# Expert weights of a two-model kernel loaded as three 2 MB transfers into three slots instead of six of 1 MB into six

## What is computed

```python
def expert_block(args):
    xblk, e = args
    return (jax.nn.silu(xblk @ w1[e]) * (xblk @ w3[e])) @ w2[e]
```

## Time and profile before

| | |
|---|---|
| median of three runs | 2905.9 us (2905.66 to 2909.65) |
| profiled execution, its own time | 2905.86 us |
| span of the profile | 2904.0 us |
| TensorE busy, matmuls | 2310.4 us, 80% |
| VectorE busy | 1070.7 us, 37% |
| ScalarE busy | 686.9 us, 24% |
| mean granted clock of TensorE | 0.900 |
| moved | 718.82 MB, mean 248 GB/s |
| share of the chain that ended last: DMA `raw<-in_w` | 24% |

### The profile page before, as it was taken

One profiled execution on the slowest core, in us unless ns is written; L12 is line 12 of the kernel. 1 busy time (PEld: TensorE's weight loads), 2 busy tenths in 40 slices (PEclk: granted clock), 3 DMA queues, 4 the chain that ended last, 5 costly groups with the idle time before them and its releaser, 6 DMA issues.

```text
span 2904.0 us, 35200 instructions
## 1 busy us (share of the span) xinstructions
PE 2310.4 (80%) x13750; PEld 1590.7 (55%) x13750; DVE 1070.7 (37%) x1570; ACT 686.9 (24%) x876; POOL 117.8 (4%) x209
## 2 busy tenths in 40 slices
PE   5998679979987699699558777877369668888885
PEld 5888478878885688587523333332355523333332
DVE  4555545555556355723420100010668410000011
ACT  3334433333335233321101000100335200000100
POOL 0001000000010000000000000000100000000000
PEclk9999789989998799899669999999679788998898
DMA  7775137757752287422149999999420269999997
GB/s 260 261 238 173 56 118 266 253 190 266 262 169 88 104 288 259 139 78 94 73 161 401 399 396 400 402 400 404 179 71 1 87 258 397 401 399 401 401 402 303
DMA packets 242628, 718.82 MB, mean 248 GB/s; under 512 B 17040, under 2 KB 156560, under 8 KB 189072
## 3 DMA queue, kind: packets, MB, share of 16 engines
q1 hardware_dynamic: 213584, 642.82, 59.7%
q10 hardware_dynamic: 19952, 48.45, 4.6%
q0 software_dynamic: 8976, 25.90, 3.0%
HBM read 693.70 MB, written 25.26 MB: 248 GB/s over the span
## 4 chain that ended last, share of the span: by engine, by line
PE 55%; DMA 26%; DVE 9%; issue 4%; DVEq 2%; ACT 2%; SPq 1%; ACTq 0%; POOL 0%; POOLq 0%
DMA raw<-in_w 24%; PE ps L620 13%; PE ps L621 12%; PE ps L622 12%; PE ps L934 10%; PE ps L655 2%; PE ps L634 1%; SPq L554 1%; PE ps L936 1%; PE ps L1071 1%; DVE t_lo L1537 1%; PE ps L1086 1%; DMA raw<-in_ffn_w_up 1%; DVE work L1601 1%; DMA work<-expert_rows,slot_of_token 1%
## 5 line engine op out<-in xcount | busy, mean ns | idle before, releaser
L1537 DVE TENSOR_TENSOR w_lo<-raw,w_hi 128x2048 fp32r<-128x2048 f32 x180 | 411.4, 2290 | 445.1 <-ACT w_hi L1128 445.1
L620 PE MATMUL ps<-t_hi,w_hi 128*128 128x256 f32 (+1 forms) x1568 | 456.4, 291 | 8.7 <-DVE t_lo L1537 8.6
L621 PE MATMUL ps<-t_lo,w_hi 128*128 128x256 f32 (+1 forms) x1568 | 454.1, 290 | 0.0
L622 PE MATMUL ps<-t_hi,w_lo 128*128 128x256 f32 (+1 forms) x1568 | 451.1, 288 | 0.0
L1128 ACT CAST w_hi<-raw 128x2048 fp32r<-128x2048 f32 x180 | 342.1, 1903 | 447.5 <-PE ps L622 428.5
L934 PE MATMUL ps<-raw,work 128*64 128x512 f32 x528 | 308.8, 742 | 167.0 <-DMA raw<-in_w 165.6
L2015 DVE COPY work<-ps 128x512 f32<-128x512 f32 x64 | 44.3, 692 | 932.6 <-PE ps L952 932.6
L620 PE MATMUL ps<-w_hi,t_hi 128*128 128x256 f32 (+1 forms) x1088 | 349.8, 322 | 15.3 <-DVE t_lo L1537 12.4
L622 PE MATMUL ps<-w_hi,t_lo 128*128 128x256 f32 (+1 forms) x1088 | 351.1, 323 | 0.0
L621 PE MATMUL ps<-w_lo,t_hi 128*128 128x256 f32 (+1 forms) x1088 | 351.0, 323 | 0.0
L620 PEld LDWEIGHTS ps<-t_hi,w_hi 128*128 128x128 f32 x1568 | 296.6, 189 | 30.4 <-issue 13.2
(11 more groups left out here) (280 smaller groups left out, 2159.1 us busy)
## 6 DMA issues: line engine op xcount, KB each, us to landing
raw<-in_w SPq DMA_DIRECT2D x256, 1024.0 KB, 11.3
work<-in_w SPq DMA_DIRECT2D x128, 1024.0 KB, 10.7
work<-in_w_mod SPq DMA_DIRECT2D x32, 1536.0 KB, 6.5
raw<-in_ffn_w_gate SPq DMA_DIRECT2D x44, 1024.0 KB, 8.8
raw<-in_ffn_w_up SPq DMA_DIRECT2D x44, 1024.0 KB, 10.3
raw<-in_ffn_w_down SPq DMA_DIRECT2D x44, 1024.0 KB, 4.9
raw<-in_w_in SPq DMA_DIRECT2D x18, 1024.0 KB, 5.5
expert_rows<-work ACTq DMA_DIRECT2D x128, 128.0 KB, 7.2
```

The costliest lines, as they stand in the source:

```text
L620: pe.matmul(dst, a[0], b[0], start=start, stop=False)
L621: pe.matmul(dst, a[0], b[1], start=False, stop=False)
L622: return pe.matmul(dst, a[1], b[0], start=False, stop=stop)
L1537: return dve.tensor_tensor(dst, src, hi.bitcast(F32), ALU.subtract)
```

## The change

The six slots of 1 MB become three of 2 MB: two from the four slots of `raw`, for w1 and w3, and one from the two in the work area, for w2. Each matrix is one transfer. SyncE waits once for the two up matrices, until the whole up product of the expert before is done (`up_done`), and once for w2, until the down product of the expert before that one in w2's order is done (`down_done`). TensorE waits once for both up matrices and once for w2; the order of its products, `expert_done` and what the other engines do are the same. The first four panels of the stage behind a loop wait for the whole last up product.

```diff
-RAW_UP = 6
+RAW_UP = 3
...
         def expert_raw(m, x):
-            return raw[:, (SPLIT_PANELS[m] + x) % RAW, :] if x < RAW else w(R3 + (x - RAW) * KD * PC, KD * PC)
+            if x < 2:
+                return raw[:, 2 * x:2 * x + 2, :].rearrange("p s n -> p (s n)")
+            return w(R3, 2 * KD * PC)
...
+        def up_done(b):
+            return 6 * b + 2 if not isinstance(b, int) or b else 4
+        def down_done(b):
+            return 6 * b + 10 if not isinstance(b, int) or b < EXPERTS - 1 else 6 * b + 6
...
-                    sp.wait_ge(expert_done, MAIN - 6 + j - G0["odd"] + 1)
+                    sp.wait_ge(expert_done, MAIN - 4)
...
-                for j in range(4):
-                    first_load(j, part((w1, w3)[j % 2], 0, j // 2))
-                for j in range(2):
-                    first_load(4 + j, part((w1, w3)[j % 2], 1, 0))
-                for j in (2, 3):
-                    expert_load(up_panel(1, j), up_slot(1, j), part((w1, w3)[j % 2], 1, 1))
-                down_loads(0, 0)
+                def load_matrix(x, wt, e, landed_in):
+                    return sp.dma_start(expert_raw(m, x).rearrange("p (a n) -> p a n", a=1), wt[:, bass.ds(e, 1), :]
+                                        ).then_inc(landed_in, 16)
+                def up_loads(e):
+                    sp.wait_ge(expert_done, MAIN * m + up_done(e - 1))
+                    for x, wt in enumerate((w1, w3)):
+                        load_matrix(x, wt, e, expert_landed[x])
+                def down_load(e):
+                    sp.wait_ge(expert_done, MAIN * m + down_done(e - 1))
+                    load_matrix(2, w2, e, expert_landed[2])
+                sp.wait_ge(w_ready, SPLIT_PANELS[m])
+                for x, wt in enumerate((w1, w3)):
+                    load_matrix(x, wt, 0, expert_landed[x])
+                sp.wait_ge(row_ready, TILE0[10 + 2 * m])
+                load_matrix(2, w2, 0, expert_landed[2])
+                up_loads(1)
                 with sp.Fori(2, EXPERTS) as e:
-                    up_loads(e, None)
-                    down_loads(e - 1, None)
-                down_loads(EXPERTS - 1, EXPERTS - 1)
+                    up_loads(e)
+                    down_load(e - 1)
+                down_load(EXPERTS - 1)
...
-                        pe.wait_ge(expert_landed[x1], count(block))
-                        pe.wait_ge(expert_landed[x3], count(block))
+                        if h == 0:
+                            pe.wait_ge(expert_landed[0], count(b))
+                            pe.wait_ge(expert_landed[1], count(b))
...
+                    pe.wait_ge(expert_landed[2], count(b))
                     for h in range(2):
-                        x = down_slot(y, h)
-                        pe.wait_ge(expert_landed[x], count(EXPERTS - 1 if y == EXPERTS - 1 else b + 1))
-                        down_half(par, h, expert_raw(m, x)).then_inc(expert_done, 1)
+                        down_half(par, h, expert_raw(m, 2)[:, h * 2048:(h + 1) * 2048]).then_inc(expert_done, 1)
```

More of the change, by code:

```diff
@@ L545, in moe @@
                 w2 = A["w2_2"][m].rearrange("e (p c) n -> p e (c n)", c=4)
[L547 to L561, removed]
@@ L563, in up_loads @@
-                def up_loads(e, x):
-                    for j in range(4):
[L565 to L571, removed]
-                    first_load(j, part((w1, w3)[j % 2], 0, j // 2))
-                for j in range(2):
-                    first_load(4 + j, part((w1, w3)[j % 2], 1, 0))
@@ L580, in moe @@
-                    down_loads(e - 1, None)
-                down_loads(EXPERTS - 1, EXPERTS - 1)
+                    up_loads(e)
+                    down_load(e - 1)
+                down_load(EXPERTS - 1)
                 def extra_loads(e):
[L585 to L590, removed]
+                    for x, wt in enumerate((w1, w3, w2)):
+                        load_matrix(x, wt, e, ex_landed[m])
@@ L961, in count @@
                 def count(y):
-                    return 16 * (EXPERTS * m + 1) + 16 * y
+                    return 16 * (b0 + 1) + 16 * y
                 def up_of(b, par, y):
@@ L970, in up_of @@
                             pe.wait_ge(xg_landed[m][1 - par], 8 * (b + par) + 16)
-                        x1, x3 = up_slot(y, 2 * h), up_slot(y, 2 * h + 1)
-                        block = b - 1 if h == 0 and (y is None or y) else b
-                        pe.wait_ge(expert_landed[x1], count(block))
-                        pe.wait_ge(expert_landed[x3], count(block))
-                        first, mm = up_half(par, h, expert_raw(m, x1), expert_raw(m, x3))
+                        if h == 0:
+                            pe.wait_ge(expert_landed[0], count(b))
+                            pe.wait_ge(expert_landed[1], count(b))
+                        first, mm = up_half(par, h, expert_raw(m, 0)[:, h * 2048:(h + 1) * 2048],
+                                            expert_raw(m, 1)[:, h * 2048:(h + 1) * 2048])
                         first.then_inc(expert_done, 1)
@@ L1023, in moe @@
                         mm.then_inc(ex_xgt[m], 1)
-                        pe.wait_ge(ex_landed[m], 96 * i + 96)
+                        pe.wait_ge(ex_landed[m], 48 * i + 48)
                         pe.wait_ge(ex_xT[m], i + 1)
                         for h in range(2):
-                            _, mm = up_half(0, h, expert_raw(m, 2 * h), expert_raw(m, 2 * h + 1))
+                            _, mm = up_half(0, h, expert_raw(m, 0)[:, h * 2048:(h + 1) * 2048],
+                                            expert_raw(m, 1)[:, h * 2048:(h + 1) * 2048])
                         mm.then_inc(ex_up[m], 1)
@@ L1032, in moe @@
                         for h in range(2):
-                            mm = down_half(0, h, expert_raw(m, 4 + h))
+                            mm = down_half(0, h, expert_raw(m, 2)[:, h * 2048:(h + 1) * 2048])
                         mm.then_inc(ex_done[m], 1)
```

## The result

The changed kernel takes 3364.6 us (median of four runs, 3359.38 to 3370.45); the kernel before took 2907.8 us beside it. The ratio is 1.157, with a 95% interval of 1.153 to 1.160: slower by 457 us, where the prediction had 3310 us, +404 and a range of 3185 to 3400.

A forecast was written before the change was run, and what follows sets the result against it. The two expert loops were taken as bound by their bytes; late release would dry the queue. Steps of 23.1 us, 31 a loop, plus 23.5 make 739.6 against 537.6, +404 for both: 3310 us, range 3185 to 3400.

The forecast's parts named there:

- The mechanism: Expert loops: w3 lands, up product, slots released, w1 and w3 refill; queue dry 6.1 us an expert, 23.1 against 17.0.
- release to issue: Expert loops: from the up product's last matmul to the next transfer's issue, 0.14 us.
- step: One expert in the loops, from one up product to the next: 23.1 us, against 17.0 before.
- What bounds the kernel: Both expert loops: an expert costs what its bytes cost, 6.82 MB at 401 GB/s, 17.0 us, with the queue full.
- Transfers and issues removed: Expert loops: three of six transfers and three issues fewer an expert, priced at nothing.
- Term 1: Up product of each expert, cold after TensorE's pause: 8.55 us, bounds 7.05 and 14.1.
- rival A: Up product: TensorE is back at full clock when it begins; 1.5 us less, 64 times, 3214 us; chance 0.12.
- Term 3: Refill of w1 and w3: fixed time of a transfer meeting an empty queue, 2.3 us, upper bound 3.1.
- the sum by the page: Refill by the skill's 2.0 us fixed cost and 436 GB/s: 0.7 us an expert less, 3270 us.
- Term 4: Refill: w1 and w3 with gather and stores beside them, 12.0 us an expert; 10.0 without that traffic.
- Rival B: Expert loops: gather and stores fill the queue's dry part, w1 and w3 take 10.0 us; 3186 us; chance 0.15.
- The ends: End of each loop, from the last up product through late-issued w2 to the last down product: 23.5 us.

The follow-up runs named there:

- Filled: Changed kernel, with TensorE multiplying the identity ten times into a free accumulator between an expert's transposes and the wait for the next weights; 3282.5 us, ratio 1.128.

## Why the prediction was right, and what it mis-sized

The mechanism was right. The number was 54 us too low: an expert costs 0.25 us more in the up product, 0.1 in the release and 0.4 in the gather and the stores, and a loop 2 us more at its end. Its terms, against the changed kernel (transposes and issues of loop 1):

| term | predicted | measured |
|---|---|---|
| up product, cold | 8.55 | 8.8 |
| release to issue | 0.14 | 0.25 |
| issue to next up product (fixed time, w1 and w3 with gather and stores, first matmul) | 14.44 | 14.9 |
| step | 23.1 | 23.9 to 24.0 |
| loop 1 | 739.6 | 767.3 |

*What bounds the kernel, and the release.* Right: with half-wise start and release, and the same bytes in fixed slots, the step is back at 17.1 us. The prediction named two parts and did not price them apart. The wait for both whole matrices before the first matmul is the larger one, 304 us (3367.4 to 3063.8), and the release of the slots as a whole is worth 130 (3063.8 to 2933.8), in this order; the release at the half with the wait for whole matrices was not run.
The sentence that the six slots hold also the first halves of the next expert was true only at the start of a loop; no term used it. And what it called 16 pairs of matmuls are pairs of records, eight pairs of matmuls; the durations were read from the records and stand.

*Transfers and issues removed: nothing.* Right, 3367 against 3365 us.

*Term 1, the clock.* Right in kind and in size. Filled, the product took 7.02 us, the loops 1.4 us an expert less, the whole 82 us less; rival A had 96. The prediction took this term as a constant. It is not one: the product grew to 9.6 us when its weights came earlier, and so the median step stayed at 23.8 to 23.9 us, whether 0.26 MB of stores or three quarters of the gather were left out.

*Term 3, the fixed time.* Right. At the end of a loop no gather is issued any more, and in the run with small stores that leaves w1 and w3 with next to nothing beside them. There they take 12.55 us from the issue to the next up product (timeline of all engines, small stores, end of loop 1):

```profile
2209.53 0.81 SPq L545 DMA_DIRECT2D raw<-in_w  x2
...
2222.08 1.08 PE L915 MATMUL ps<-raw,work 128*64 128x512 f32 x1 [7.46 <-DMA raw<-in_w]
```

My rows gave 2.3 + 10.0 + 0.14 = 12.4 us for it. There was some luck in that: the transfer of the earlier trace rows from which the 2.3 us were read was not alone, as the prediction has it. It is the first of two that were issued within 0.81 us (timeline of SyncE's queue, kernel before):

```profile
1426.87 0.81 SPq L561 DMA_DIRECT2D work<-in_w  x2
```

By the fixed cost and the rate in the section on the anatomy of one DMA, "DMA: Bandwidth & Descriptors" of the Trainium skill, w1 and w3 would take 11.6 us, an estimate; the page's fit is for GpSimd's path, and these rows don't bear it out for SyncE's; the sum by the page, 3270 us, lay further from the measured time than mine.

*Term 4, the traffic beside w1 and w3.* This was mis-sized. I took an expert's whole traffic less w2 at the rate of before, 12.0 us, that is 2.0 for gather and stores over the 10.0 of the weights. They cost 2.4: 14.9 us in the loop against the 12.55 without both. Most of it is the gather. In the last two steps of loop 1 the changed kernel has stores but no gather and needs 12.9 and 13.1 us (below, 2216.79 to 2229.89), some 1.9 less than in the loop; the run with a quarter of the gather and the full clock gained 84 us; and the six slices of the DMA view at 189 to 357 GB/s instead of 430 are 1.2 to 1.3 us, on top of the time of the gather's own bytes. The stores make up the other 0.4 to 0.5 us. Why both cost more here than the 2.0 us that I took from before stays open. Rival B, that both find the dry part, is refuted: the gather's slices lie behind the dry ones in the DMA view, and the stores are issued at 1721.21, when the weights flow again.

*The ends.* Predicted 23.5 us from the last up product of a loop to its end; measured 25.6 (2229.89 to 2255.5). Of the 2.1 us, 1.3 are the last down product, which runs cold too, 4.98 us instead of 3.65:

```profile
2216.79 0.81 SPq L545 DMA_DIRECT2D raw<-in_w  x2
...
2229.89 1.09 PE L915 MATMUL ps<-raw,work 128*64 128x512 f32 x1 [8.01 <-DMA raw<-in_w]
...
2250.51 4.98 PE L933 MATMUL ps<-work 128*64 128x512 f32 x16 [8.03 <-DMA work<-in_w]
```

Together: 31 steps of 0.8 us more are 26 us a loop, the end 2, two loops 55: 404 and 55 are 459, measured 457. None of the versions beats the kernel before, whose loops are bound by their bytes.

## What to carry to other kernels

Before merging buffers or transfers, write down the cycle from a landing through the work that frees the slot to the next landing, and compare it with the transfer time of what else is queued meanwhile. If the work that frees the slot, plus the start of a new transfer, is longer than the rest of the queue, the queue runs dry; here 8.8 + 0.25 + 2.3 us against 5.0 us of w2. With the queue dry in every expert the count of transfers and their size (1 or 2 MB) didn't matter, their release and the wait of the first matmul did. For a queue that stays full this is not shown: no run with 2 MB transfers came back to 17.0 us an expert.

## What was not expected of the hardware

The step of a chain that pauses TensorE for some 9 to 10 us an expert had a median of 23.8 to 23.9 us in four kernels, with all stores and gathers, with small stores and with a quarter of the gather. With the quarter gather the up product lengthened by most of what the transfers shortened (8.8 and 14.9 us became 9.6 and 13.6). Here a saving on the transfer side showed in full only when the clock was held at 1.00: 22 us with the clock falling, 84 us without. And a gather of 0.26 MB took about 1.3 us of weight transfer for three quarters of its rows, more than the 0.5 us of their bytes at 400 GB/s, while 0.26 MB of stores cost about 0.4 us.
